# The last eight row sums of the modulation weights: from layer 1's input projection to its output projection

## The reference

```
mod = silu(c) @ w_mod[l] + b_mod[l]            # six vectors of 1024: shift, scale, gate, twice
h   = rms_norm(x, g_norm1) * (1 + sc1) + sh1
z   = h @ w_in                                 # input projection, four head groups
y   = concat(global attention, windowed attention, GLA, mLSTM) @ w_out
x   = x + ga1 * y                              # output projection and gated residual
x   = x + ga2 * (relu((rms_norm(x, g_norm2) * (1 + sc2) + sh2) @ w_mlp1) ** 2) @ w_mlp2
```

## Time and profile before

| | us |
|---|---|
| median of 3 runs | 1897.63 (1896.71 to 1899.12) |
| profiled execution | 1898.77 |
| its span | 1897.0 |
| TensorE busy | 1749.9 (92%) |
| VectorE busy | 1206.9 (64%) |
| ScalarE busy | 814.3 (43%) |
| GpSimd busy | 258.9 (14%) |

### The profile page before, as it was taken

The page is one execution under the profiler, slowest core; times in us unless marked ns, Lnnn a source line. Parts: engine busy times, 40 slices in busy tenths (PEclk is TensorE's granted clock), DMA queues, the critical chain, the costliest instruction groups (busy, mean ns, idle before and its releaser), DMA issues.

```text
span 1897.0 us, 29114 instructions
## 1 busy us (share of the span) xinstructions
PE 1749.9 (92%) x11904; PEld 1548.7 (82%) x11904; DVE 1206.9 (64%) x1761; ACT 814.3 (43%) x1178; POOL 258.9 (14%) x184
## 2 busy tenths in 40 slices
PE   6999999888897999999999978999888979999998
PEld 4778897668786989999899958778677768989897
DVE  5373636666528797896987955564666386647472
ACT  5433325543316633535435453333552365445261
POOL 0334623000210000000000033453100300000000
PEclk9899999998998999999999989999999979999999
DMA  9441113000055527458175123221200236455341
GB/s 371 154 159 45 46 45 134 2 1 1 23 180 221 221 103 304 160 189 310 66 276 221 44 70 128 91 76 56 111 2 1 111 124 253 147 208 211 122 178 45
DMA packets 43518, 247.18 MB, mean 130 GB/s; under 512 B 5604, under 2 KB 7050, under 8 KB 24714
## 3 DMA queue, kind: packets, MB, share of 16 engines
q1 hardware_dynamic: 43402, 245.55, 34.9%
HBM read 218.79 MB, written 26.74 MB: 129 GB/s over the span
## 4 chain that ended last, share of the span: by engine, by line
PE 69%; DVE 13%; ACT 6%; issue 5%; POOL 3%; DMA 3%; POOLq 0%; DVEq 0%; SPq 0%; ACTq 0%
PE ps L3221 19%; PE ps L3184 10%; PE ps L2907 8%; PE ps L2730 7%; PE ps L3143 5%; POOL w_lo L806 2%; PE ps L2987 2%; PE ps L2657 2%; DMA raw<-w_big 1%; DVE xT L2426 1%; PE ps L3102 1%; DMA raw<-w_modl 1%; PE ps L3033 1%; DVE w_lo L2380 1%; PE ps L3040 1%
## 5 line engine op out<-in xcount | busy, mean ns | idle before, releaser
L3221 PE MATMUL ps<-op_hi,w_hi 128*128 128x384 f32 x896 | 307.6, 343 | 21.8 <-DVE xT L2426 9.0
L806 POOL TENSOR_TENSOR w_lo<-raw,w_hi 128x512 fp32r<-128x512 f32 x124 | 175.2, 1444 | 955.9 <-ACT w_hi L912 933.5
L3221 PE MATMUL ps<-op_lo,w_hi 128*128 128x384 f32 x896 | 304.4, 340 | 0.0
L3221 PE MATMUL ps<-op_hi,w_lo 128*128 128x384 f32 x896 | 304.1, 339 | 0.0
L3221 PEld LDWEIGHTS ps<-op_hi,w_hi 128*128 128x128 f32 x896 | 170.6, 190 | 29.5 <-issue 26.9
L3221 PEld LDWEIGHTS ps<-op_lo,w_hi 128*128 128x128 f32 x896 | 171.0, 191 | 0.0
L3221 PEld LDWEIGHTS ps<-op_hi,w_lo 128*128 128x128 f32 x896 | 170.9, 191 | 0.0
L1387 ACT ACTIVATE w_hi<-raw 128x1024 fp32r<-128x1024 f32 x80 | 84.5, 1058 | 149.1 <-PE ps L3221 141.0
L2907 PE MATMUL ps<-w_hi,h_hi 128*128 128x256 f32 x448 | 133.5, 298 | 5.6 <-POOL w_lo L806 5.6
L3143 PE MATMUL ps<-op_hi,w_hi 128*128 128x256 f32 x448 | 128.3, 286 | 9.9 <-DVE hid L2281 6.2
L1323 ACT ACTIVATE w_hi<-raw 128x1024 fp32r<-128x1024 f32 x72 | 74.0, 1053 | 144.7 <-PE ps L3184 126.2
(11 more groups left out here) (370 smaller groups left out, 4066.0 us busy)
## 6 DMA issues: line engine op xcount, KB each, us to landing
raw<-w_big SPq DMA_DIRECT2D x96, 1024.0 KB, 6.3
raw_m<-w_modl SPq DMA_DIRECT2D x21, 1024.0 KB, 5.6
op_hi<-op_cache SPq DMA_DIRECT2D x21, 768.0 KB, 4.7
op_lo<-op_cache SPq DMA_DIRECT2D x21, 768.0 KB, 6.2
raw<-w_modl SPq DMA_DIRECT2D x14, 1024.0 KB, 4.9
op_hi<-op_cache SPq DMA_DIRECT2D x21, 512.0 KB, 4.0
op_lo<-op_cache SPq DMA_DIRECT2D x21, 512.0 KB, 5.1
first_mod<-w_modl SPq DMA_DIRECT2D x8, 1024.0 KB, 21.1
```

The source lines that it names most:

```text
L806: ins = nc.gpsimd.tensor_tensor(w_lo[r][:, ks, :], raw[0][:, ks, :], w_hi[r][:, ks, :].bitcast(F32), ALU.subtract)
L3221: ins = mm(bank(base + g, 0, h), wide(w)[:, k, g * P:(g + 1) * P], ops[hl][:, k, 0:h], start=(p in FRESH and k == 0 and q == 0), stop=(k = ...
```

## The change

The eight row sums move from the input projection to the output projection of layer 1. Rows 0 and 1 are done after `add_square` of k = 3, rows 2 to 4 after k = 4, rows 5 to 7 after k = 5, followed by `row_bias`. All eight blocks and `row_c` are loaded at once, into buffers of their own (free at that time), by nine DMAs that SP issues after the last weight slot and ahead of blocks "21" and "22". The wait of block "12" for the row sums goes.

```
-ROW_AT = (4, 8, 17, 21, 25, 29, 33, 37)
+LAST_ROWS = 8
+ROWS_BEHIND = {3: (0, 1), 4: (2, 3, 4), 5: (5, 6, 7)}
...
-    row_w = raw[1][:].rearrange("p k m -> p (k m)")[:, 0:D_MODEL]
-    row_c = raw[1][:].rearrange("p k m -> p (k m)")[:, D_MODEL:2 * D_MODEL]
+    rows_at = [RH + i * D_MODEL * 4 for i in range(6)] + [RS + i * D_MODEL * 4 for i in range(2)]
+    last_row = [place(f"last_row{i}", a, [D_MODEL]) for i, a in enumerate(rows_at)]
+    row_c = place("row_c", RV + HB1, [D_MODEL])
...
-                    for i, q in enumerate(ROW_AT):
-                        if l == 1 and i > 0 and (q - 1) // 4 == s:
-                            load_row(M_ROWS + i)
...
                     sp.wait_ge(sem("big_done"), slot_done(w0 + IN_SLOTS))
+                    sp.dma_start(row_c[:], cs_row.to_broadcast([P, D_MODEL])).then_inc(slot_landed(3), 16)
+                    for x, group in enumerate(ROWS_BEHIND.values()):
+                        for i in group:
+                            at = i % 2 * D_MODEL
+                            sp.dma_start(last_row[i][:], w_mod[MODS_1 + (M_ROWS + i) // 2][:, at:at + D_MODEL]).then_inc(
+                                slot_landed(3 + x), 16)
                     block1("21", 0)
                     block1("22", 0)
                     sp.wait_ge(sem("lo_ready"), 2 * PROJ)
                     block1("11", 0)
-                    sp.wait_ge(sem("row_done"), ROWS)
                     block1("12", 0)
...
-                sp.dma_start(row_c, cs_row.to_broadcast([P, D_MODEL])).then_inc(sem("row_landed"), 16)
-                load_row(M_ROWS)
...
-                if l == 1 and q in ROW_AT:
-                    i = ROW_AT.index(q)
-                    dve.wait_ge(sem("row_landed"), 16 * (2 + M_ROWS // 2 + 1 + i + 1))
-                    row_sum(row_w, row_c, m_first + M_ROWS + i)
-                    if i == len(ROW_AT) - 1:
-                        row_bias(M_ROWS, ROWS)
+            def rows_behind(l, k):
+
+                if l == 0 or k not in ROWS_BEHIND:
+                    return
+                dve.wait_ge(slot_landed(3 + list(ROWS_BEHIND).index(k)), 16 + 48)
+                for i in ROWS_BEHIND[k]:
+                    row_sum(last_row[i][:], row_c[:], m_first + M_ROWS + i)
+                if k == 5:
+                    row_bias(M_ROWS, ROWS)
...
                     residual(l, n_t, k, 16)
                     add_square(k, n_t)
+                    rows_behind(l, k)
```

More of the change, by code:

```diff
@@ L57 @@
 ROW_SLOTS = (0, 2, 4, 5)
-ROW_AT = (4, 8, 17, 21, 25, 29, 33, 37)
-ROWS = M_ROWS + len(ROW_AT)
+LAST_ROWS = 8
+ROWS_BEHIND = {3: (0, 1), 4: (2, 3, 4), 5: (5, 6, 7)}
+ROWS = M_ROWS + LAST_ROWS
 A_PHASES = 7
@@ L541, in load_w @@
                 wts.add()
[L543 to L548, removed]
             def load_block(name, i, part):
```

## The result

The changed kernel took 1905.74 us (median of 20 runs, 1902.23 to 1911.44); the kernel before, run beside it, 1899.71 us (20 runs, 1896.53 to 1904.83). The ratio is 1.0032, with a 95% interval of 1.0023 to 1.0042: slower by 6.1 us (4.4 to 8.0). The forecast was 1907.0 us in a range of 1902 to 1912.5. The profiled execution took 1903.53 us, its span is 1901.8 us.

The account below looks back on a forecast made before the run. TensorE carried 69% of the chain, but the output projection ended with block "11"'s landing plus a fixed tail. Input projection -2.1, "11" +7.8 and three sums +3.7 made +9.4 us: 1907.0 against median 1897.63, range 1902 to 1912.5.

Parts of the forecast that it names:

- Gain of the input projection, -2.1: Layer 1's input projection: without row sums TensorE's waits for snap and sacc go, 0.9, 0.9 and 0.2 us.
- the 10.7 us of the chain: Rival, input projection: it gives back what its chain shows, 10.7 us, not TensorE's waits; 1898.4 us, 4%.
- Block "11", +7.8: Layer 1's output projection: block "11" queues behind the row data, landing at 1,522.9 in place of 1,515.04, +7.8 us.
- the pile at the start: Kernel's start: 14.45 MB of queued transfers at 404 GB/s, taken as nearest case for the landing of "11".
- the slow row data of the rival: Rival, output projection: row data come slower or SP's queue is full, "11" lands 13 us late; 1912 us, 10%.
- Three sums on the chain, +3.7: Output projection: rows 5 to 7 and row_bias between add_square k=5 and residual k=6 are not hidden, +3.7 us.
- Five sums hidden: Output projection: rows 0 to 4, after k=3 and k=4, are covered by the wait for "11"; delay at most 0.5.
- From the norm on nothing: From the norm behind the output projection on: same durations as before, nothing added; a loss of 1 us possible.
- ACT's wait for "11": Output projection, sign in the profile: ACT's w_hi waits about 14 us for its raw block instead of 6.96.
- The sum, +9.4: Whole kernel: -2.1 + 7.8 + 3.7 = +9.4 us, giving 1907.0 us against the median 1897.63.
- The two cases "not slower": Rivals: "11" isn't held up, 1899.5 us, 6%; input projection gives back what its chain shows, 1898.4 us, 4%.
- the low edge of the forecast's case: Whole kernel: lower end of the forecast case's own range, 1903 to 1910 us; that case has 77%.

Follow-up runs that it names:

- the respaced rows (row 5 at step 31): Kernel before with row sums 2, 4, 5 and 6 at steps 20, 27, 31 and 35 in place of 17, 25, 29 and 33: 1896.20 us, ratio 0.9985.
- the kernel with neither: Changed kernel with one row block loaded and eight sums of only 8 elements reading it: 1894.39 us, ratio 0.9967 to the kernel before.
- the tiny sums: Changed kernel with each late row sum reading 8 of 1,024 elements, all nine loads kept: 1903.77 us, ratio 1.0015 to the kernel before.
- the sums put ahead: Changed kernel with rows 5 to 7 and the bias moved from behind add_square k=5 to behind k=4: 1903.73 us, ratio 1.0018 to the kernel before.
- the sums alone: Changed kernel with one row block loaded in place of eight, all eight full sums reading it: 1899.70 us, ratio 0.9995 to the kernel before.
- the two with the sums ahead: Changed kernel with rows 5 to 7 behind k=4: 1903.73 us; the same with block "11" issued ahead of "21" and "22": 1900.45 us.
- the three with respaced rows: Kernel before with sums at other input projection steps: row 5 at step 29, 1894.78 and again 1897.31 us; at step 31, 1896.20 us.

## Why the prediction was right, point by point

- **Gain of the input projection, -2.1.** -2.36 in each of the seven profiles without row sums there: 1.10 at `snap` (forecast 0.94), 0.97 at the second `sacc` (0.9), 0.27 at the last (0.2). That only what TensorE waited for comes back, and not the 10.7 us of the chain, is shown twice: by these, and by the respaced rows (row 5 at step 31), which get the same 2.36 with all DVE work left in. That rival falls. (The timed -6.3 us, -8.7 to -3.6, of the kernel with neither excludes its 10.7 us as well, though it lies beyond the 2.4 us too.)
- **Block "11", +7.8.** It landed 26.0 us after the last slot's issue in place of 17.6: +8.4. That the row data do it is shown by the runs with and without the sums' data: with seven of the eight blocks gone it landed after 19.3 us, and the 1.7 us above the 17.6 are POOL's late split, which counts only when the queue is free. The rate held (379 to 429 GB/s against 404 taken), and so did the pile at the start as the nearest row; the slow row data of the rival did not come. The Trainium skill, page "DMA: Bandwidth & Descriptors", section "Anatomy of one DMA", has a sum for one transfer on the path that GpSimd issues, 2.0 us plus bytes at 436 GB/s; used for the whole pile of 8.91 MB it is an estimate of 22.4 us after the slot's issue. It measured 26.0, so the measurement decides for a pile of thirteen transfers that SyncE issued on one queue.
- **Three sums on the chain, +3.7.** 4.36 us from `add_square` k=5 to residual k=6, in place of 0.61: +3.75. Shown by the tiny sums, which took 3.2 us off it, and by the sums put ahead, which took this price away whole.
- **Five sums hidden.** Right: rows 0 and 1 ended at 1,504.61 and rows 2 to 4 at 1,510.09; counted from the stage's start as before (7.07 us later) that is 1,511.7 and 1,517.2, where about 1,512 and 1,517 were forecast. TensorE waited 0.3 us for residual k=4 (forecast at most 0.5).
- **From the norm on nothing.** Right within 0.4 us. TensorE stood still for 15.52 us (about 16 forecast); its granted clock was 0.50, that is 1.2 GHz, at the norm as before, and 0.63 in the mean already over 1,521 to 1,525.
- **A sign that was off.** ACT's wait for "11" was given as about 14 us and came out 10.39, since ACT's square in front of it was itself held by residual k=4, which came behind rows 0 and 1. The landing and the sum are not touched: a wait's length depends on its start too.
- **The sum, +9.4.** The stages make +9.8, the timed comparison +6.1 (4.4 to 8.0), the changed kernel's second one +8.0 (4.8 to 11.2). The forecast difference was 3.3 us too large against the first and 1.4 against the second. The predicted time, 1907.0 against 1905.74, came nearer than that by luck: it was built on a median of three runs, 1897.63, that lies 2.1 us under that of the 20, and the two errors offset each other.
- **A slip in the chances.** The two cases "not slower" were given 6% and 4%, yet together with the low edge of the forecast's case they are said to make 8%. It should have been 10% at least. The sum and the bounds of the range don't use it.

**What stays open.** The timed differences lie under the sums of the two stages nearly everywhere: by 3.7 us in the first comparison of the changed kernel, 1.7 in the second, 3.3 with the loads alone, 4.0 with the sums alone, 3.9 with neither, 2.2 and 4.2 in the two with the sums ahead. For the kernel before against itself it is 2.0, for the three with respaced rows 1.1, -0.4 and 0.4. The intervals are 1.8 to 3.2 us to each side, so no single one says much, but the seven kernels without rows in the input projection show some 3 us and the four with them about 1. A gain of up to 2 us elsewhere, in execution that isn't profiled, can't be excluded. The profiles show none: up to 1,198 us the differences between them have both signs. Much of the scatter goes with the granted clock. Of 64 runs of the kernel before on one chip (both rounds), the 27 with a mean granted clock of 0.966 or more have a median of 1897.14 us, the 25 with 0.963 or less one of 1903.43. For the kernel with neither (mean 0.966, against 0.965 in the 30 runs of before beside it) that is an estimated 1 us of its gap of 3.9; the rest is unexplained. It wasn't tried further.

## What to carry to other kernels

Before work is moved out of a stage, ask how much of it the bounding engine waits for there: 1.1, 1.0 and 0.3 us here, out of eight sums of 1.1 to 2.3 us. Moving four of the sums two or three steps within the stage gave back the same 2.4 us and cost nothing that a profile shows, where moving them to another stage cost 12 us. A stage whose bounding engine has room can still end in a transfer; data put ahead of that transfer on its queue delay it by bytes over rate (4.7 MB at 0.40 MB/us is 11.7 us, less the time for which the queue stood idle before). And work parked in a wait is free only as long as the wait is: when "11" was brought forward by 4.8 us, the six sums in its shadow took 3.6 of them back.

## What the runs showed of the hardware that was not expected

- A DVE sum of 8 elements took 1.23 us beside POOL and 0.16 us without it. The first ran from 1,504.08 to 1,505.31; the POOL instruction that had started just before it ended at 1,505.29:

```profile
1504.00 1.29 POOL L801 TENSOR_TENSOR w_lo<-raw,w_hi 128x512 fp32r<-128x512 f32 x1
```

So the price of meeting POOL is not in proportion to the DVE work. The Trainium skill, page "SBUF — State Buffer", section "SBUF: two separate sides", says that of a DVE operation with two SBUF inputs and a GpSimd one that reads SBUF, the one that starts first holds the shared ports for its whole instruction and the other is blocked; the trace agrees.

- POOL pays as well: its four split instructions took 5.49 us with the tiny sums, 5.95 before, 6.48 in the changed kernel and 7.46 where both sums ran wholly beside it.
- A lower clock can hide in a wait: with 0.50 in place of 0.72 granted over 1,230 to 1,236 us, TensorE took 1.2 us more up to the merge behind them, its wait of 0.94 us for that merge was gone, and the stage took 0.17 us more in all.
- One kernel's position at the start of layer 1 differs by 3.7 us between two profiles that differ in nothing (the changed kernel: -3.89 and -0.20), and over all kernels, alike up to there but for a load or two, by 9 us. It goes mostly with the clock: over the first 1,093 us the mean granted clock was 0.98 in the profile that came there first (1,093.38) and 0.96 in the one that came last (1,102.54, the kernel with neither). A single pair of profiles must be compared stage by stage.
